# Recurrence of a WKV layer: block-diagonal scores over both chunks, and the next tile's decays earlier in the order

## The reference, cut to what matters

```
def wkv7_scan(r, decay, k, kk, a, v):
    def step(state, inp):
        r_t, w_t, k_t, kk_t, a_t, v_t = inp
        sa = jnp.einsum('bhvk,bhk->bhv', state, -kk_t)
        state = (state * w_t[:, :, None, :]
                 + sa[..., None] * (kk_t * a_t)[:, :, None, :]
                 + v_t[..., None] * k_t[:, :, None, :])
        return state, jnp.einsum('bhvk,bhk->bhv', state, r_t)
...
    y = wkv7_scan(r_h, heads(decay), k_h, kk, heads(a), v_h)
    mean = jnp.mean(y, axis=-1, keepdims=True)
    var = jnp.mean(jnp.square(y - mean), axis=-1, keepdims=True)
    y = ((y - mean) * lax.rsqrt(var + GN_EPS)).reshape(b, s, RWKV_WIDTH)
```

## Time and profile before

| | us |
|---|---|
| median of 3 runs | 4269.78 |
| lowest and highest | 4264.81, 4272.55 |
| the profiled execution | 4274.97 |
| its span | 4273.0 |

### The profile page before, as it was taken

One profiled execution on the slowest core, in us unless ns is written; L12 is line 12 of the kernel. 1 busy time (PEld: TensorE's weight loads), 2 busy tenths in 40 slices (PEclk: granted clock), 3 DMA queues, 4 the chain that ended last, 5 costly groups with the idle time before them and its releaser, 6 DMA issues. The chain is left out here.

```text
span 4273.0 us, 53547 instructions
## 1 busy us (share of the span) xinstructions
PE 3314.9 (78%) x20733; PEld 2665.5 (62%) x20733; DVE 1810.8 (42%) x2500; ACT 1149.3 (27%) x1433; POOL 689.5 (16%) x340
## 2 busy tenths in 40 slices
PE   7999767878547599579999877999965645645489
PEld 7999656767424344358888633999964534534277
DVE  2000054543366422458888633200015764566321
ACT  2000022222123211157777512200004113221211
POOL 2332141311000000122222100223202311110000
PEclk9999867777557699789999988999985656766789
DMA  4221210100111242379999743222231021021321
GB/s 144 104 86 69 103 53 22 41 21 7 34 50 40 106 184 89 121 260 399 399 399 399 272 159 126 83 94 95 81 98 59 0 75 50 0 75 31 129 74 59
DMA packets 238047, 500.70 MB, mean 117 GB/s; under 512 B 34528, under 2 KB 103344, under 8 KB 236736
## 3 DMA queue, kind: packets, MB, share of 16 engines
q1 hardware_dynamic: 184592, 381.62, 24.8%
q10 hardware_dynamic: 43536, 82.91, 5.4%
q0 software_dynamic: 9776, 34.16, 2.2%
HBM read 393.52 MB, written 99.75 MB: 115 GB/s over the span
## 5 line engine op out<-in xcount | busy, mean ns | idle before, releaser
L340 PE MATMUL pin_psum<-pin_sb_w,pin_sb_hT 128*128 128x354 f32 (+1 forms) x5376 | 975.0, 343 | 25.4 <-DVE pin_sb_w L304 22.8
L340 PEld LDWEIGHTS pin_psum<-pin_sb_w,pin_sb_hT 128*128 128x128 f32 x5376 | 936.1, 189 | 61.1 <-DVE pin_sb_w L304 23.6
L3524 DVE TENSOR_TENSOR moe_sb_wlo<-moe_sb_raw,moe_sb_whi 128x2048 fp32r<-128x2048 f32 x192 | 437.8, 2286 | 93.6 <-ACT moe_sb_whi L3349 93.5
L321 DVE TENSOR_SCALAR pin_sb_xt<-pin_psum,pin_sb_ss 128x353 f32<-128x353 f32 (+1 forms) x112 | 70.0, 628 | 835.8 <-PE pin_psum L340 835.6
L3349 ACT ACTIVATE moe_sb_whi<-moe_sb_raw 128x2048 fp32r<-128x2048 f32 x192 | 367.3, 1916 | 134.8 <-DMA moe_sb_raw<-in_w_gate 46.9
L278 ACT ACTIVATE pin_sb_xt<-pin_psum,pin_sb_ss 128x353 f32<-128x353 f32 (+1 forms) x112 | 65.4, 590 | 832.0 <-PE pin_psum L340 831.4
L3592 PE MATMUL moe_psum<-moe_sb_whi,moe_sb_xhi 128*128 128x512 f32 x512 | 204.7, 400 | 15.9 <-DVE moe_sb_xlo L3528 15.9
L3592 PE MATMUL moe_psum<-moe_sb_wlo,moe_sb_xhi 128*128 128x512 f32 x512 | 201.4, 393 | 0.0
L3592 PE MATMUL moe_psum<-moe_sb_whi,moe_sb_xlo 128*128 128x512 f32 x512 | 201.3, 393 | 0.0
L239 POOL TENSOR_TENSOR pin_sb_w<-pin_sb_raw,pin_sb_w 128x2832 fp32r<-128x2832 f32 (+1 forms) x26 | 182.3, 7013 | 3.9 <-issue 0.2
L237 POOL CAST pin_sb_w<-pin_sb_raw 128x2832 fp32r<-128x2832 f32 (+1 forms) x26 | 75.0, 2884 | 653.2 <-PE pin_psum L340 604.5
(11 more groups left out here) (647 smaller groups left out, 5693.1 us busy)
## 6 DMA issues: line engine op xcount, KB each, us to landing
moe_sb_raw<-in_w_gate SPq DMA_DIRECT2D x64, 1024.0 KB, 13.9
moe_sb_raw<-in_w_up SPq DMA_DIRECT2D x64, 1024.0 KB, 14.1
moe_sb_raw<-in_w_down SPq DMA_DIRECT2D x64, 1024.0 KB, 13.1
pin_sb_raw<-in_w_in SPq DMA_DIRECT2D x16, 1412.0 KB, 6.3
scratch_proj<-pin_sb_xt ACTq DMA_DIRECT2D x16, 1412.0 KB, 6.2
...
```

The source lines that it names most:

```text
L321: v.tensor_scalar(og[b][:, t, :], ps[:, t, 0:width], ss[:, 3, t:t + 1], None, ALU.mult).then_inc(dve_free, 1)
L340: mm = te.matmul(ps[:, t, 0:cols], hT[a_part][:, k, t * P:(t + 1) * P], wt[b][w_part][:, k, :], start=(k == 0 and n == 0), stop=(k == KD - ...
L3524: tt(wlo[q][:, :, :], raw[q][:, :, :], whi[q][:, :, :].bitcast(F32), ALU.subtract).then_inc(lo, 1)
```

## The change

It does five things.

1. **Block-diagonal scores.** Km, QB and QK become 128x128 a head, zero outside the two chunk blocks. VectorE fills each by two half-height instructions (`blocked`, 64 rows of 8x64) in place of one of full height. The zeros, and Us, are set once at the start. `state_rows` and `state_out` then take all 128 rows in every product, and pick the chunk by the column half of the stationary side.
2. **Decays forward.** On VectorE `decays(t+1)` stands before the carried state of chunk 1, lm (`sums_shifted`) before x32 and `scale` before `centred` and xf. On ScalarE `decays`, `gate` and `norm` stand before XX8, `exps` before the Z64 eviction, and `norm_square` and `root` last. `sums` on PE is split, the column sums for pend being `ends`, with steps of their own.
3. **PE's list of the recurrence** is moved back: `state_out` of chunk 0 behind mn4, the four steps of chunk 1 one place later each, `state_out` of chunk 1 between z64 and xf.
4. **New waits.** The transposes of ka wait for the xf of the tile before, since bank 3 holds its product. `state_step` of chunk 0 and `carried` wait for pend. n64 is masked after X1 and its step is now waited for ahead of the qk scores.
5. **GpSimd's shift** is cut into four pieces of 448 columns.

The core of the diff:

```diff
-        Km, QB, QK, XF = (two(n, G8) for n in ("Km", "QB", "QK", "XF"))
+        XF = two("XF", G8)
+        Km, QB, QK = (two(n, [P, RH, P]) for n in ("Km", "QB", "QK"))
...
-                    mm = te.matmul(ps[o, STEP, d], Km[b][o, hp(h), :], vv[b][o, d], start=False, stop=True)
+                    mm = te.matmul(ps[o, STEP, d], Km[b][:, hp(h), o], vv[b][:, d], start=False, stop=True)
...
-                    te.matmul(ps[o, OUT, d], QB[b][o, hp(h), :], Us[o, h, :], start=False, stop=False)
-                    mm = te.matmul(ps[o, OUT, d], QK[b][o, hp(h), :], vv[b][o, d], start=False, stop=True)
+                    te.matmul(ps[o, OUT, d], QB[b][:, hp(h), o], Us[:, h, :], start=False, stop=False)
+                    mm = te.matmul(ps[o, OUT, d], QK[b][:, hp(h), o], vv[b][:, d], start=False, stop=True)
...
+            def blocked(t, stage, src, outs, step):
+                ve.drain()
+                ve.wait_ge(pe.sem, pe.at(stage, t))
+                for dst, slot, m in outs:
+                    for c in range(2):
+                        o = half(c)
+                        ins = tt(dst[o, :, o].rearrange("p (q i) c -> p q i c", q=2), split(src, slot)[o], m24(m)[o], ALU.mult)
+                ins.then_inc(dve.sem, dve.step(step))
...
+                    if m == 3 and not first(t):
+                        te.wait_ge(dve.sem, dve.at("xf", t - 1))
+                        te.sem_inc(passed, 1)
...
+            cuts = [slice(448 * i, 448 * i + 448) for i in range(4)]
...
-                tt(prev[:, :], prev[:, :], x[:, :], ALU.subtract)
+                for c in cuts:
+                    tt(prev[:, c], prev[:, c], x[:, c], ALU.subtract)
```

More of the change, by code:

```diff
@@ L1066, in rwkv @@
         passed = ph.sem("passed")
-        fa = ph.steps("front_act", "lora_in square decays gate norm enl exps lmexp")
+        fa = ph.steps("front_act", "lora_in square decays gate norm enl el lmexp pend")
         fd = ph.steps("front_dve", "xs loT kk wp ap ss lm scaled")
-        fp = ph.steps("front_pe", "lora_t wp ap gate sums")
+        fp = ph.steps("front_pe", "lora_t wp ap gate sums ends")
         act = ph.steps("act", "arT mn2 mn4 xx8 z32 z64")
-        dve = ph.steps("dve", "n64 qb x1 qk bsum x2 x4 in8 x32 xt32 xf")
-        pe = ph.steps("pe", "turned mn kq qk mn2 x2 mn4 x4 n8 xx8 z32 x32 xt32 z64 xf")
+        dve = ph.steps("dve", "qb x1 n64 qk bsum x2 x4 in8 x32 xt32 xf")
+        pe = ph.steps("pe", "turned mn kq mn2 qk x2 mn4 x4 n8 xx8 z32 x32 xt32 z64 xf")
         pool = ph.steps("pool", "rk bonus")
@@ L1189, in body @@
                 evict(t, "mn4", flat2(MN4), pair(1))
+                if not last(t):
+                    decays(t + 1)
+                    gate(t + 1, 1 - b)
+                    norm(t + 1)
                 if not first(t):
                     state_copy(t - 1, 1, "r", Rs)
+                evict(t, "xx8", flat2(XX8), pair(1))
+                if not first(t):
                     state_copy(t - 1, 1, "u", Us)
-                evict(t, "xx8", flat2(XX8), pair(1))
-                if not last(t):
-                    decays(t + 1)
                 evict(t, "z32", one(Z32), ps[:, 3, :])
-                if not last(t):
-                    gate(t + 1, 1 - b)
-                if not last(t):
-                    norm(t + 1)
-                if not first(t):
-                    norm_square(t - 1)
-                evict(t, "z64", one(Z64), ps[:, 2, :])
-                if not first(t):
-                    root(t - 1)
                 if not last(t):
@@ L1209, in body @@
                     exps(t + 1, 1 - b)
+                evict(t, "z64", one(Z64), ps[:, 2, :])
+                if not first(t):
+                    norm_square(t - 1)
+                    root(t - 1)
             for c in (fa, act, sa, na):
@@ L1429, in body @@
                     variance(t - 1)
-                if more:
-                    scale(t + 1, 1 - b)
-                if not first(t):
                     output(t - 1, 1 - b)
             ve.memset(Sst[:, :, :], 0.0)
-            for z in Sbd:
+            for z in (*Sbd, *Km, *QB, *QK, Us):
                 ve.memset(z[:, :, :], 0.0)
@@ L1577, in body @@
                 prod(3, M1, N1).then_inc(pe.sem, pe.step("mn2"))
-                if not first(t):
-                    te.wait_ge(nd.sem, nd.start(t - 1))
-                    te.sem_inc(passed, 1)
-                    state_out(t - 1, 1 - b, 0)
+                te.wait_ge(dve.sem, dve.at("n64", t))
+                te.sem_inc(passed, 1)
+                score(0, 0, kaT, rhT).then_inc(pe.sem, pe.step("qk"))
                 if more:
@@ L1590, in body @@
                 prod(2, M2, N2).then_inc(pe.sem, pe.step("mn4"))
-                if not first(t):
-                    state_rows(t - 1, 1 - b, 1)
                 if more:
                     lora_a(t + 1)
+                if not first(t):
+                    te.wait_ge(nd.sem, nd.start(t - 1))
+                    te.sem_inc(passed, 1)
+                    state_out(t - 1, 1 - b, 0)
                 te.wait_ge(act.sem, act.at("mn4", t))
@@ L1615, in body @@
                 if not first(t):
-                    state_out(t - 1, 1 - b, 1)
+                    state_step(t - 1, 1 - b, 1)
+                if more:
+                    sums(t + 1)
                 te.wait_ge(act.sem, act.at("z32", t))
@@ L1621, in body @@
                 if more:
-                    sums(t + 1)
+                    ends(t + 1)
                 te.wait_ge(dve.sem, dve.at("x32", t))
@@ L1625, in body @@
                 prod(2, N64, X32).then_inc(pe.sem, pe.step("z64"))
+                if not first(t):
+                    state_out(t - 1, 1 - b, 1)
                 te.wait_ge(act.sem, act.at("z64", t))
```

61 lines of the change are left out of this document (37 added, 24 removed).

## The result

| kernel | median, us | runs | profiled execution, us | its span, us |
|---|---|---|---|---|
| before | 4270.66 | 4264.81 to 4272.55 | 4274.97 | 4273.0 |
| changed | 4113.77 | 4108.22 to 4115.15 | 4114.64 | 4112.6 |

The ratio is 0.9634, with a 95% interval from 0.9617 to 0.9650. Between the two profiled executions lie 160.3 us; 4130 was forecast for the profiled execution and 4125 for the median.

What follows compares the result with a forecast made beforehand. TensorE work, partly at half clock, plus its waits bound the recurrence. Six tiles -120, tile 0 -3, tile 7 -10, tail -12: -145, 4274.97 to 4130 profiled, 4125 us median; range 4072 to 4190.

Steps and rivals of the forecast that it cites:

- Row height: state_rows and state_out: uniform 128-row products take 0.11 us each at full rate, saving 9.6 us a tile.
- The end waits: PE at a tile's end: waits for the Z64 eviction (4.87) and next scaled inputs (7.05) go, 11.9 us.
- The work, 35.4: PE in a steady tile: full-rate work falls from 45 us by 9.6 to 35.4.
- The new waits, 13.1 a tile: PE in a steady tile: waits for ka, arT, u0 copy, QB, n64, QK and XX8 sum to 13.1 us.
- The clock, 2.5 a tile left over: PE in a steady tile: work at half rate adds 2.5 us, making the tile 51.0.
- Tail: Recurrence of tile 7 alone at the end, at half rate all through: -12 us.
- Tile 7: Last tile, clock 0.83: row height saves 9.6 us, new waits about equal those that go; -10 us.
- Row height not the price: Rival: 9.6 us a tile and the tail stay, 60.6 us a tile, 4203 us; chance 0.04.
- Slower by the clock: Rival: clock stays at 0.5 for the whole phase, 74.6 us a tile, 4299 us; chance 0.03.
- New waits for old: Rival: VectorE's early chain is longer, clock stays 0.74, 59.5 us a tile, 4181 us; chance 0.15.
- All hidden at full clock: Rival: no GpSimd/VectorE lock, clock 1, 43.5 us a tile, about 4065 us; chance 0.12.
- The signs: Profile: heads 0.22 and 0.33 us apart, no PE wait over 1 us before xf and transposes, clock 0.8 or more.

Runs made afterwards that it cites:

- grouped64: Changed kernel with 64-row Km, QB, QK products, grouped behind the Sbd products in state_rows and state_out, accumulation left out; 4112.2 us, one run.
- u_first: Changed kernel with the copy of u0 ahead of lora_in on ScalarE; 4108.3 us, ratio 0.9627 to the kernel before.
- changed_again: The changed kernel measured once more, with nothing altered; 4106.5 us, ratio 0.9617 to the kernel before.
- rows64: Changed kernel with the Km, QB and QK products 64 rows high again, all else kept; 4193.2 us, ratio 0.9813 to the kernel before.
- carried_late: Changed kernel with the copy of u0 ahead of lora_in (ScalarE) and carried(0) behind x2 and the bias of wp (VectorE); 4084.2 us, ratio 0.9566 to before.
- scale_late: Changed kernel with the next tile's scaling products back behind centred, xf and variance on VectorE; 4142.4 us, ratio 0.9701 to the kernel before.
- qk_first: Changed kernel with the QK masks ahead of carried(0) on VectorE; 4108.9 us, ratio 0.9633 to the kernel before.
- front_late: Changed kernel with the next tile's shifted behind the N32 and N64 masks, LoRA steps later, carried(0) behind x2; 4112.2 us, ratio 0.9629 to before.

## Why the prediction held, step by step

**Row height: right, 9.1 us a tile at full rate where 9.6 stood.** The new products have 0.117 us at full rate and 0.21 at half, as taken from state_solve. That the price lies in the change of height is now shown (grouped64) and no longer an inference.

**The end waits: right.** Both are gone, in the six tiles and at tile 1. VectorE ended the scaling products at 804.8, before PE's xf at 805.24.

**The split of a tile: errors that cancelled, which is luck.** The total of a tile was right to 0.3 us, 50.7 for 51.0. To compare the terms, PE's busy time in slices of 0.5 us is weighted with the clock of each slice; what it would take at full rate is the work, the rest is the cost of half rate (us a tile):

| term | before, as predicted from | before, by slices | forecast | changed, by slices |
|---|---|---|---|---|
| work at full rate | 45 | 44.2 | 35.4 | 37.9 |
| cost of half rate | 13 | 13.7 | 2.5 | 5.5 |
| waits | 13.0 | 13.0 | 13.1 | 7.3 |
| tile | 71.0 | 71.0 | 51.0 | 50.7 |

The waits came out 5.8 us too long, the work 2.5 and the clock 3.0 too short.

- *The work, 35.4, measured 37.9.* The 45 us came from halving the busy time at half rate. A head that changes height takes 0.80 or 1.02 us there, not twice 0.52 or 0.63, so halving counts 0.12 too little for each head that ran at half rate, at most 3.8 us for the 32 heads of a tile. From such a 45 the saving at full rate, 9.6, could not be taken in full.
- *The new waits, 13.1 a tile, measured 7.35.* QK was put at 4.9 and took 2.8. Of the difference 1.3 lie in carried, where the hold-up by GpSimd's pieces was put at 3 us for three instructions and is 1.7: the pair takes 1.70 instead of 0.85 and the next one (Sst) 1.24 instead of 0.42. The rest was not separated. The copy of u0 was put at 3.2 and took 7.5 us in six tiles, 1.25 each: it shares one cause with QB (u_first), and I had chained them as if each added. arT (1.4) took 0.3, ka (0.7) 0.1, and n64 (1.1) nothing; QB, 1.5, took 1.25. Against that stand 1.35 a tile of issue time, for which I had no term at all.
- *The clock, 2.5 a tile left over, was 5.5.* The reason given, that no wait over 5 us is left, does not carry: the clock falls inside shorter waits too. In changed_again PE waits 2.49 us for the copy of u0 (until 763.01) and 4.24 us for QK (until 775.64), and a low stretch begins in each (slices of 1 us, the clock is the third number from the end):

```profile
761.00:762.00 1.00, 0.00 (x0) 0.00 (x0) 0.90 (x1) 0.07 (x1) 0.00 (x0) 1.00 0.46 176
...
763.00:764.00 1.00, 0.99 (x18) 1.00 (x20) 0.85 (x2) 0.00 (x0) 0.00 (x0) 0.50 0.88 186
...
770.00:771.00 1.00, 1.00 (x24) 0.50 (x16) 0.96 (x1) 0.94 (x1) 1.00 (x2) 1.00 0.00 0
...
773.00:774.00 1.00, 0.00 (x0) 0.00 (x0) 0.96 (x1) 0.00 (x0) 0.86 (x2) 0.50 0.00 0
```

The start of a tile, on the other hand, which the prediction let stay low with the transposes, has a clock of 1.00 in the changed kernel in the first 1.7 us of tiles 1, 2, 4 and 6 (from 602.26, 650.26, 755.09 and 858.07); tile 3, behind 3.48 us of idle time, starts at 0.50.

**What goes with the clock.** In the same order it is 0.82 with alternating heights (rows64), 0.87 and 0.88 without (changed, grouped64). In carried_late, with 10 us less of idle time, it is 0.93: the QK waits are nearly gone, and PE's busy time at half rate is 35 us in six tiles, where the changed kernel has 66 and scale_late, with 30 us more of idle time, 63. But the sum of the idle time does not set it: u_first, qk_first and front_late have 0.90 and 0.91 with as much idle time as the changed kernel. Where the waits lie seems to count, but this was not tested by itself, and each of these values is from one profile. Why the clock fell in the kernel before in state_out with PE busy throughout is not shown by any run.

**Tail: -18.6 where -12 stood.** The step that failed is "at half rate all through". At half rate the gain is 11.1 (grouped64); the changed kernel's tail rose to the full level for part of it, a mean of 0.75, which I had only in the rival. **Tile 7:** -8.3 for -10, but not by its terms: PE's busy time fell by 12.9 us, with the clock going from 0.83 to 0.96, and its waits grew from 4.0 to 8.6, where the prediction had the clock and the waits as they were. **Tile 0:** -4.1 for -3, and tile 0 took between 36.1 and 39.2 us in runs that leave it as it is, so no more can be read from it.

**The rivals.** Row height not the price: out, by rows64 and grouped64. Slower by the clock: out, 0.87. New waits for old: out in the sum; in kind it was right, for VectorE's early chain is what PE waits for. All hidden at full clock, 43.5 a tile: carried_late, with one step of that chain moved, stands at 46.7.

**The signs.** Heads, QB and QK masks, u0 copy and clock as listed. The pair was to be 2 to 3 us and was 1.70. "No wait over 1 us before the transposes" holds for what has a releaser and fails for issue, 3.48 and 2.88 us. Tiles were 48.0 to 54.9, against 48 to 55.
